# RWKV-7 scan on one Trainium2 core: carried state joined in PSUM by an identity product, new state written by ScalarE

## The chip, the cores and the metric

The kernel runs on one NeuronCore of one Trainium2 chip. The metric is the device time of one execution in microseconds (us), lower is better. Besides the timed executions there is one profiled execution, whose trace gives the start and length of every instruction on TensorE (PE for its matmuls, PEld for its weight loads), VectorE (DVE), ScalarE (ACT), GpSimd (POOL) and of the DMA queues issued by SyncE (SP).

## The reference, cut to what matters

The program is one step of a four-layer decoder trunk on 512 prompt tokens and 8 sample tokens, in float32. The second layer mixes tokens with RWKV-7: 16 heads, each with a 64x64 state matrix S that every token updates.

```python
def step(S, inp):
    r_t, w_t, k_t, v_t, kk_t, a_t = inp
    sa = jnp.einsum('bhvk,bhk->bhv', S, -kk_t)
    S = (S * w_t[:, :, None, :] + sa[..., None] * (kk_t * a_t)[:, :, None, :]
         + v_t[..., None] * k_t[:, :, None, :])
    return S, jnp.einsum('bhvk,bhk->bhv', S, r_t)

S, y = lax.scan(step, S0.astype(jnp.float32), (tm(rh), tm(decay), tm(kh), tm(vh), tm(kk), tm(ah)))
```

The other three layers (short convolution, gated linear attention, short convolution) and the feed-forward part behind each layer are not touched by the change.

## The kernel before, in words

**The scan.** The 512 prompt tokens are cut into 8 chunks of 64 (`NCH = 8`), and the 16 heads into two halves (`q` = 0 and 1) of four partition pairs: two heads of 64 channels lie one above the other in the 128 partitions, and index `i` runs over the four pairs. One scan step handles one chunk of one half, so there are 16 steps, numbered `w = 2 * c + q`. With decays taken relative to the start of a chunk, the step needs a triangular inverse of a 64x64 matrix per head, which it builds in five levels (2, 4, 8, 16, 32), then a right side, a solution `uu`, the outputs of the chunk and the new state.

**The rows of work.** TensorE's program is written out for all 16 steps. All its small products go through `both` (L2094), which issues one 64x64 matmul per head (line L2097 in the profile). In the trace every such float32 matmul shows as two records, so one call of `both` is four MATMUL records and four LDWEIGHTS records. Some products stay on the partitions they read ("diagonal"), others write the other head's partitions (`far`).

**One step in TensorE's order** (`scan_step`, L2203): the update products of level 0; the outputs of the previous step's solution (`outputs_of_solution`, rows `sc,uu`); the previous step's state sums (`state_products`, rows `uu,tok` and `tok`, eight calls of `both` into bank 7), which end with the semaphore `st_mm`; the first score products of the next step (rows `bd_B,bd_ZR`, `bd_ZR,bd_B`, `bd_ZR,bd_K`); the first products of level 1 (rows `mmt,ct`), and so on level by level.

**Around it.** In each level TensorE's first product (`t1_mm`) is copied out by ScalarE (`t`, L1405), TensorE makes the update products (rows `t,mmt` and `mmt,t`), VectorE adds them into `mmt` (L2920), and the next level's first products wait for that and for a masked matrix `ct` of GpSimd (L895). VectorE also masks the next step's scores (L2886), builds its operands (L2865, L2866, L2871, L2877) and walks through the sample tokens' state update (L2836 to L2850). GpSimd makes the next step's first inverse (L886, L888). ScalarE further writes the exponentials (L1363, L1364), `tok` (L1386, L1392), `uu` (L1433) and the outputs (L1436).

**The state.** `rw_ST` holds the state transposed. At the end of each step VectorE computes `st_end`, old state times end decay (L2942). When `st_mm` has come, VectorE writes the new state as (sums in bank 7) times end decay plus `st_end`, in four SCALAR_TENSOR_TENSOR (`update_state`, L2893), and copies the next end decay (`end_decays`, L2882), then waits for that copy before it masks the next scores.

**Order.** Each engine runs its instructions in the order in which the code writes them; only semaphores tie the engines together. There is no planner.

## Time and profile before

| | us |
|---|---|
| median of 3 timed runs | 3038.99 |
| lowest and highest | 3037.69, 3041.12 |
| span of the profiled execution | 3035.3 |
| the scan in it: first to last `rw_ST` write | 930.0 to 1133.6 |
| TensorE busy in the span | 2890.8 (95%) |
| VectorE busy | 1541.5 (51%) |
| ScalarE busy | 1051.5 (35%) |
| GpSimd busy | 1335.8 (44%) |

The trace gives no time of the profiled execution other than its span, first to last instruction; the median of the timed runs is 3.7 us above it.

In rows of the trace the first number is a start or a share as each heading says; `x4` is a count; `[0.24 <-PE banks L2097]` is idle time of the engine just before the row and what ended it. "issue" means that the engine waited for nothing that the profile shows. Consecutive instructions of an engine overlap, so the distance between starts, not the length, says what one costs in a row.

### The profile page before, as it was taken

The page shows a single profiled execution, that of the slowest core. Times are in us where ns is not written, and L with a number is a line of the kernel's source. Part 1 is how long each engine was busy: PE and PEld are TensorE (multiplying, and loading weights), DVE is VectorE, ACT ScalarE, POOL GpSimd, SP SyncE. Part 2 cuts the span into 40 slices and gives each one's busy share as a digit, 9 for nine tenths or more (in the row PEclk, how much of TensorE's full clock was granted, in tenths as well). Part 3 has the DMA queues.
Part 4 walks back from the last instruction along what each step waited for, and adds up shares of the span by engine and source line. Part 5 has one row for each costly group of instructions (what it writes and reads, how often), then busy time and mean ns, then how long its engine had stood idle before and what let it go on. Part 6 is the DMA issues. An engine that isn't in the chain of part 4 may idle for free.

```text
span 3035.3 us, 74569 instructions
## 1 busy us (share of the span) xinstructions
PE 2890.8 (95%) x30385; PEld 2739.4 (90%) x30385; DVE 1541.5 (51%) x2144; ACT 1051.5 (35%) x2059; POOL 1335.8 (44%) x981
## 2 busy tenths in 40 slices
PE   6998999998989899999998999989999999899998
PEld 6998999997978777899997899879999899799998
DVE  3435666128358884666603151476650444566612
ACT  4224333225454342433323443243332422433322
POOL 3443444442435564344443263434444344354443
PEclk8999999999999999999999899999999999899999
DMA  7544333543310014333344313433334443233332
GB/s 268 165 153 160 92 91 91 166 131 130 118 43 18 4 25 126 122 91 91 101 154 157 98 56 118 157 124 91 91 112 149 163 127 91 59 96 89 92 90 85
DMA packets 465625, 332.67 MB, mean 110 GB/s; under 512 B 19914, under 2 KB 435608, under 8 KB 465122
## 3 DMA queue, kind: packets, MB, share of 16 engines
q1 hardware_dynamic: 461400, 325.24, 34.5%
q10 hardware_dynamic: 4010, 4.22, 0.6%
q8 instruction: 178, 2.92, 0.4%
q14 instruction: 37, 0.30, 0.0%
HBM read 319.62 MB, written 10.20 MB: 109 GB/s over the span
## 4 chain that ended last, share of the span: by engine, by line
PE 57%; issue 4%; DVE 4%; POOL 3%; ACT 2%; DMA 1%; SPq 0%; POOLq 0%; ACTq 0%; DVEq 0%
PE banks L1638 33%; PE banks L1646 16%; POOL ct L895 2%; PE banks L2097 1%; PE banks L1599 1%; DVE h L2622 1%; PE banks L1944 1%; DVE proj L2566 1%; PE banks L1661 1%; POOL mmt L886 0%; PE banks L1732 0%; DMA s_state<-in_state_wkv_b_dram 0%; ACT conv L1074 0%; POOL mmt L888 0%; PE banks L2291 0%
## 5 line engine op out<-in xcount | busy, mean ns | idle before, releaser
L766 POOL TENSOR_TENSOR w_lo<-w_raw,w_hi 128x1024 fp32r<-128x1024 f32 x395 | 1007.3, 2551 | 1115.7 <-ACT w_hi L975 1095.7
L1638 PE MATMUL banks<-u_hi,w_hi 128*128 128x260 f32 x4064 | 836.8, 287 | 13.9 <-ACT w_hi L975 9.4
L1638 PE MATMUL banks<-u_lo,w_hi 128*128 128x260 f32 x4064 | 827.4, 285 | 0.0
L1638 PEld LDWEIGHTS banks<-u_hi,w_hi 128*128 128x128 f32 x4064 | 629.4, 190 | 27.1 <-issue 15.2
L1638 PEld LDWEIGHTS banks<-u_lo,w_hi 128*128 128x128 f32 x4064 | 632.1, 190 | 1.8
L975 ACT ACTIVATE w_hi<-w_raw 128x1024 fp32r<-128x1024 f32 x402 | 424.8, 1057 | 456.5 <-PE banks L1646 290.1
L1646 PE MATMUL banks<-u_hi,w_lo 128*128 128x260 f32 x4064 | 528.5, 283 | 0.0
L1646 PEld LDWEIGHTS banks<-u_hi,w_lo 128*128 128x128 f32 x4064 | 502.5, 187 | 1.8
L1638 PE MATMUL banks<-hid_hi,w_hi 128*128 128x260 f32 x1664 | 336.3, 283 | 0.0
L1638 PE MATMUL banks<-hid_lo,w_hi 128*128 128x260 f32 x1664 | 335.2, 283 | 0.0
L3069 DVE TENSOR_TENSOR csb<-proj 128x520 f32 (+1 forms) x42 | 30.3, 722 | 470.8 <-ACT proj L1042 470.8
L2554 DVE TENSOR_TENSOR hid_lo<-prod,hid_hi 128x520 f32 x104 | 261.6, 2516 | 12.8
L1638 PEld LDWEIGHTS banks<-hid_hi,w_hi 128*128 128x128 f32 x1664 | 256.8, 188 | 5.0 <-issue 3.7
L2538 DVE SCALAR_TENSOR_TENSOR conv<-gate,vecs,conv 128x536 f32<-128x536 f32 x104 | 249.1, 2395 | 15.1 <-DVE conv L2536 0.8
L1638 PEld LDWEIGHTS banks<-hid_lo,w_hi 128*128 128x128 f32 x1664 | 256.0, 188 | 0.0
L1646 PE MATMUL banks<-hid_hi,w_lo 128*128 128x260 f32 x1664 | 217.0, 282 | 0.0
L1646 PEld LDWEIGHTS banks<-hid_hi,w_lo 128*128 128x128 f32 x1664 | 206.4, 188 | 0.0
L781 POOL TENSOR_TENSOR tail<-gate,ones 128x2 f32<-128x2 f32 x104 | 27.1, 260 | 339.8 <-ACT gate L1507 339.8
L1514 ACT ACTIVATE conv<-conv,vecs 128x536 f32<-128x536 f32 x88 | 65.6, 745 | 287.5 <-DVE conv L2538 287.5
L2535 DVE TENSOR_SCALAR conv<-gate,vecs 128x536 f32<-128x536 f32 x104 | 56.0, 538 | 194.4 <-ACT gate L1507 190.3
L895 POOL TENSOR_TENSOR ct<-sc,head_up 128x128 f32<-128x128 f32 x160 | 92.3, 593 | 85.1 <-PE banks L2097 84.9
L1505 ACT ACTIVATE gate<-banks 128x260 f32<-128x260 f32 x88 | 34.1, 388 | 257.5 <-PE banks L1646 256.3
(461 smaller groups left out, 3903.9 us busy)
## 6 DMA issues: line engine op xcount, KB each, us to landing
w_raw<-in_ffn_w_up_dram SPq DMA_DIRECT2D x176, 512.0 KB, 3.6
ada_raw<-in_ada_w_dram SPq DMA_DIRECT2D x96, 512.0 KB, 4.8
w_raw<-in_ffn_w_down_dram SPq DMA_DIRECT2D x64, 448.0 KB, 3.8
w_raw<-in_sconv_w_in_dram SPq DMA_DIRECT2D x48, 512.0 KB, 5.3
ada_ahead<-in_ada_w_dram SPq DMA_DIRECT2D x36, 512.0 KB, 7.6
ada_ahead_down<-in_ada_w_dram SPq DMA_DIRECT2D x36, 512.0 KB, 6.4
w_raw<-in_ffn_w_down_dram SPq DMA_DIRECT2D x32, 512.0 KB, 4.1
ada_pro<-in_ada_w_dram SPq DMA_DIRECT2D x6, 2048.0 KB, 20.3
```

The source lines that it names most:

```text
L766: pool.tensor_tensor(w_lo[:, s, :, :], w_raw[:, s, :, :], w_hi[:, s, :, :].bitcast(F32), ALU.subtract).then_inc(lo_done, 1)
L895: pool.tensor_tensor(ct[:, 2 * g:2 * g + 2, :], sc[q][:, 2 * g:2 * g + 2, HD:2 * HD], m, ALU.mult).then_inc(ct_ready, 1)
L975: act.activation(w_hi[:, s, :, :], w_raw[:, s, :, :], ACT.Copy).then_inc(hi_done, 1)
L1505: act.activation(gate[:, e, 2:2 + HALF], tile_ps[0][0][:, 0:HALF], ACT.Copy)
L1514: act.activation(conv[:, e, 0:CWD], conv[:, e, 0:CWD], ACT.Silu, bias=vec("ffn_conv_b", l * FT + m)).then_inc(silu_done, 1)
L1599: mm = pe.matmul(acc_ps[g * QUAD:(g + 1) * QUAD, 0:2 * P], cT[:, k, :], parts[:, g, :, :], start=(k == 0), stop=(k == KT - 1))
L1638: pe.matmul(tile_ps[slot][half][0:width, 0:HALF], w_hi[:, s, k, 0:width], x[:, k0 + k, half * HALF:(half + 1) * HALF], start=start and k = ...
L1646: mm = pe.matmul(tile_ps[slot][half][0:width, 0:HALF], w_lo[:, s, k, 0:width], xh[:, k0 + k, half * HALF:(half + 1) * HALF], start=False, ...
L1661: pe.matmul(tile_ps[s][half][:, 0:HALF], w[:, s, k, :], xh[:, k, half * HALF:(half + 1) * HALF], start=(start and k == 0 and i == 0), stop ...
L2535: link(dve.tensor_scalar(conv[:, e, 0:CWD], gate[:, e, 0:CWD], w[0], None, ALU.mult))
L2538: dve.scalar_tensor_tensor(conv[:, e, 0:CWD], gate[:, e, 2:2 + CWD], w[2], conv[:, e, 0:CWD], ALU.mult, ALU.add).then_inc(conv_done, 1)
L2554: dve.tensor_tensor(lo, prod[:, e, :], hi.bitcast(F32), ALU.subtract).then_inc(hid_ready, 1)
```

## The change

Three things change in the scan. First, `state_products` on TensorE gets a third call of `both` per pair: identity times the old `rw_ST`, accumulated into the same sums in bank 7. Second, the new state is then those sums times the end decay alone; ScalarE writes it, as four ACTIVATE copies whose scale is a 128x1 column of `end_decay`, placed ahead of the level-1 copies of the step. Third, VectorE loses `st_end` and `update_state`; its copy of the end decay moves to level 2 of the step, behind a wait for `st_updated`, and signals a new semaphore `decays_ready`. ScalarE's loop is rewritten so that its first step stands outside.

```diff
-        st_end = at("st_end", [P, 4, HD], F32, big_off + 5 * 1024)
...
+                    def update_state(w, q):
+
+                        act.wait_ge(st_mm, w + 1)
+                        act.wait_ge(decays_ready, w + 1)
+                        for i in range(4):
+                            ins = act.activation(rw_ST[:, 4 * q + i, :], bank[7][:, i * HD:(i + 1) * HD], ACT.Copy,
+                                                 scale=end_decay[:, q, i:i + 1])
+                        ins.then_inc(st_updated, 1)
+
-                    def scan_step(c, q, one_more, two_more):
+                    def scan_step(c, q, one_more, two_more, first=False):
 
                         w = 2 * c + q
+                        if not first:
+                            update_state(w - 1, 1 - q)
                         for lvl in range(1, len(LEVELS)):
...
                             both(o, lambda rs: tok[q][rs, i, 0:HD], lambda rs: uu[rs, i, :], True, False)
-                            mm = both(o, lambda rs: tok[q][rs, i, HD:2 * HD], lambda rs: tok[q][rs, i, 2 * HD:3 * HD], False, True)
+                            both(o, lambda rs: tok[q][rs, i, HD:2 * HD], lambda rs: tok[q][rs, i, 2 * HD:3 * HD], False, False)
+                            mm = both(o, lambda rs: ident[rs, rs], lambda rs: rw_ST[rs, 4 * q + i, :], False, True)
                         mm.then_inc(st_mm, 1)
...
-                    def update_state(w, q, two_more):
-
-                        dve.wait_ge(st_mm, w + 1)
-                        for i in range(4):
-                            ins = dve.scalar_tensor_tensor(rw_ST[:, 4 * q + i, :], bank[7][:, i * HD:(i + 1) * HD],
-                                                           end_decay[:, q, i:i + 1], st_end[:, i, :],
-                                                           ALU.mult, ALU.add)
-                        ins.then_inc(st_updated, 1)
-                        if two_more:
-                            dve.wait_ge(st_updated, w + 3)
-                            link(end_decays(q))
...
-                            if lvl == 0 and not first:
-                                update_state(w - 1, 1 - q, one_more)
...
-                            elif lvl == 2 and two_more:
-                                dve.wait_ge(exp_done, w + 3)
-                                dve.wait_ge(rhs_mm, w + 1)
-                                build(c + 1, q)
+                            elif lvl == 2:
+                                if one_more and not first:
+                                    dve.wait_ge(st_updated, w + 2)
+                                    end_decays(1 - q).then_inc(decays_ready, 1)
+                                if two_more:
+                                    dve.wait_ge(exp_done, w + 3)
+                                    dve.wait_ge(rhs_mm, w + 1)
+                                    build(c + 1, q)
...
-                        dve.wait_ge(st_updated, w + 1)
-                        dve.wait_ge(st_updated, w + 2)
-                        link(dve.tensor_tensor(st_end[:, :, :], rw_ST[:, 4 * q:4 * q + 4, :],
-                                               end_decay[:, q, :].unsqueeze(2).to_broadcast([P, 4, HD]), ALU.mult))
```

On TensorE, in a step with q = 0, the state sums of the step before stood like this (each row of "x2" is one call of `both`, `uu` is the solution, `tok` keys and values, `bd_` rows are the scores that follow):

```order
L2097 MATMUL banks<-uu,tok_139 64x64 x2
L2097 MATMUL banks<-tok_139 64x64 x2
L2097 MATMUL banks<-uu,tok_139 64x64 x2
L2097 MATMUL banks<-tok_139 64x64 x2
L2097 MATMUL banks<-bd_B_123,bd_ZR_122 64x64 [waits bd_ready]
L2097 MATMUL banks<-bd_B_123,bd_ZR_122 64x64
L2097 MATMUL banks<-bd_ZR_122,bd_B_123 64x3x64 x2
L2097 MATMUL banks<-bd_ZR_122,bd_K_124 64x3x64 x2
L2097 MATMUL banks<-mmt_136,ct 64x64 [waits mmt_ready,ct_ready]
```

and in the changed program, where `both` is at L2110, the same place of a step reads:

```order
L2110 MATMUL banks<-uu,tok_139 64x64 x2
L2110 MATMUL banks<-tok_139 64x64 x2
L2110 MATMUL banks<-rw_ST,ident 64x64 x2
L2110 MATMUL banks<-uu,tok_139 64x64 x2
L2110 MATMUL banks<-tok_139 64x64 x2
L2110 MATMUL banks<-rw_ST,ident 64x64 x2
L2110 MATMUL banks<-bd_B_128,bd_ZR_127 64x64 [waits bd_ready]
L2110 MATMUL banks<-bd_B_128,bd_ZR_127 64x64
L2110 MATMUL banks<-bd_ZR_127,bd_B_128 64x3x64 x2
L2110 MATMUL banks<-bd_ZR_127,bd_K_129 64x3x64 x2
L2110 MATMUL banks<-mmt_134,ct 64x64 [waits mmt_ready,ct_ready]
```

Each pair has gained one call of `both` ahead of the scores and of the level-1 products (`mmt,ct`); nothing behind it changed its order.

On VectorE, behind the level-0 additions of a step, the program before has the new state, the end decay with its waits, then the first mask (`sc`) and the level-1 additions:

```order
L2920 TENSOR_TENSOR mmt_136<-mmt_136,banks 128x256 [waits tok_ready,d_mm]
L2893 SCALAR_TENSOR_TENSOR rw_ST<-banks,end_decay,st_end 128x64 [waits st_mm]
L2893 SCALAR_TENSOR_TENSOR rw_ST<-banks,end_decay,st_end 128x64 x3
L2898 REGISTER_ALU
L2882 COPY end_decay<-bd_Ep_126 128x4 [waits st_updated]
L2464 ISA
L2885 ISA [waits dve_step]
L2886 TENSOR_TENSOR sc_133<-banks,sc_mask 128x320 [waits sc_done]
```

and the changed program goes from the additions to the mask at once:

```order
L2921 TENSOR_TENSOR mmt_135<-mmt_135,banks 128x256 [waits tok_ready,d_mm]
L2898 ISA
L2899 TENSOR_TENSOR sc_132<-banks,sc_mask 128x320 [waits sc_done]
L2909 REGISTER_ALU
L2921 TENSOR_TENSOR mmt_135<-mmt_135,banks 128x256 [waits mmt_ready,d_mm]
```

The end decay's copy has moved two levels down, between the mask and the operands of level 2.

On ScalarE, the program before goes from the outputs' copy (`rw_kk`) to the level-1 copies (`t`):

```order
L1436 ISA [waits y_mm]
L1436 ACTIVATE rw_kk<-banks 128x4x64
L1404 REGISTER_ALU
L1405 ACTIVATE t_138<-banks 128x128 [waits t1_mm]
L1404 REGISTER_ALU
L1405 ACTIVATE t_138<-banks 128x128 [waits t1_mm]
```

and the changed program has the new state between them:

```order
L1446 ISA [waits y_mm]
L1446 ACTIVATE rw_kk<-banks 128x4x64
L1410 REGISTER_ALU
L1413 ACTIVATE rw_ST<-banks,end_decay 128x64 [waits decays_ready,st_mm]
L1413 ACTIVATE rw_ST<-banks,end_decay 128x64 x3
L1403 ISA
L1404 ACTIVATE t_137<-banks 128x128 [waits t1_mm]
```

So the level-1 copies now stand behind a wait for `st_mm` and four more instructions.

## Rows read from the trace of the kernel before

**Rows 1.** The page, part 1, busy time and share of each engine.
```profile
PE 2890.8 (95%) x30385; PEld 2739.4 (90%) x30385; DVE 1541.5 (51%) x2144; ACT 1051.5 (35%) x2059; POOL 1335.8 (44%) x981
```

**Rows 2.** Busy time by stretch, the 15 scan steps, columns as headed.
```profile
core 0: us, PE busy (x) PEld busy (x) DVE busy (x) ACT busy (x) POOL busy (x), PEclk, DMA share, GB/s
926.00:1133.00 207.00, 188.78 (x6487) 169.24 (x6479) 174.88 (x422) 86.48 (x319) 125.22 (x212) 0.99 0.02 6
```

**Rows 3.** Waits in the same stretch: waiter, releaser, us in total, times, longest.
```profile
PEld banks L2097 <- issue: 20.5, 41, 1.8
DVE rw_ST L2893 <- PE banks L2097: 8.7, 16, 1.4
PE banks L2097 <- POOL mmt L888: 5.2, 7, 0.9
PE banks L2097 <- DVE mmt L2920: 2.6, 4, 1.7
PEld banks L2097 <- ACT t L1405: 1.4, 7, 0.2
```

**Rows 4.** PE's timeline in one step: start, length, instruction, count, idle before.
```profile
981.83 0.25 PE L2097 MATMUL banks<-sc,uu 64*64 64x64 f32 x1
...
982.33 0.22 PE L2097 MATMUL banks<-uu,tok 64*64 64x64 f32 x1
...
983.26 0.22 PE L2097 MATMUL banks<-bd_B,bd_ZR 64*64 64x64 f32 x1
...
983.45 0.27 PE L2097 MATMUL banks<-mmt,ct 64*64 64x64 f32 x2
```

**Rows 5.** DVE's timeline in the same step.
```profile
982.30 0.74 DVE L2920 TENSOR_TENSOR mmt<-mmt,banks 128x256 f32<-128x256 f32 x2
983.54 0.86 DVE L2893 SCALAR_TENSOR_TENSOR rw_ST<-banks,end_decay,st_end 128x64 f32<-128x64 f32 x4 [0.50 <-PE banks L2097]
984.43 0.17 DVE L2882 COPY end_decay<-bd_Ep 128x4 f32<-128x4 f32 x1
984.76 0.49 DVE L2886 TENSOR_TENSOR sc<-banks,sc_mask 128x320 f32<-128x320 f32 x1 [0.16 <-DVE end_decay L2882]
985.49 0.75 DVE L2920 TENSOR_TENSOR mmt<-mmt,banks 128x256 f32<-128x256 f32 x2 [0.24 <-PE banks L2097]
```

**Rows 6.** ACT's timeline in the same step, solution and level-1 copies.
```profile
981.30 0.38 ACT L1433 ACTIVATE uu<-banks 128x256 f32<-128x256 f32 x1 [0.20 <-PE banks L2097]
984.40 0.45 ACT L1405 ACTIVATE t<-banks 128x128 f32<-128x128 f32 x2 [1.32 <-PE banks L2097]
```

**Rows 7.** ACT's lengths by line: ns min/median/max; copies without and with a column scale.
```profile
L1386 ACT ACTIVATE tok<-banks x64: 266/273/285, 908.8 to 1114.4; 128x128 f32<-128x128 f32 x64
L1398 ACT ACTIVATE mmt<-banks x16: 384/384/386, 913.9 to 1116.0; 128x256 f32<-128x256 f32 x16
L1424 ACT ACTIVATE bonus_ones<-pair_ones,vecs x8: 389/392/403, 1119.6 to 1126.7; 128x128 f32<-128x128 f32 x8
```

**Rows 8.** ACT's timeline, last step: two scaled copies in a row.
```profile
1119.27 0.48 ACT L1405 ACTIVATE t<-banks 128x128 f32<-128x128 f32 x2 [0.64 <-PE banks L2097]
1119.64 0.68 ACT L1424 ACTIVATE bonus_ones<-pair_ones,vecs 128x128 f32<-128x128 f32 x2
```

**Rows 9.** DVE's timeline, last step: its own new state.
```profile
1119.18 0.86 DVE L2893 SCALAR_TENSOR_TENSOR rw_ST<-banks,end_decay,st_end 128x64 f32<-128x64 f32 x4 [1.05 <-PE banks L2097]
```

**Rows 10.** DMA queues in 926 to 1133: packets, MB, share.
```profile
q8 instruction: 52, 0.85, 1.6%
```

**Rows 11.** Timeline behind the scan, PE.
```profile
1130.88 0.42 PE L2097 MATMUL banks<-uu,tok 64*64 64x64 f32 x4
...
1132.65 1.98 PE L2283 MATMUL banks<-rw_kk,pair_ones 128*128 128x512 f32 x4
...
1134.73 1.10 PE L2097 MATMUL banks<-ident,rw_ST 64*64 64x64 f32 x32
```

**Rows 12.** DVE's length of the old state's product, ns min/median/max.
```profile
L2942 DVE TENSOR_TENSOR st_end<-rw_ST,end_decay x16: 410/420/1105, 926.5 to 1128.7; 128x256 f32<-128x256 f32 x16
```

**Rows 13.** GpSimd's first inverse, a step with q = 1, then one with q = 0.
```profile
964.51 0.90 POOL L886 TENSOR_TENSOR mmt<-sc,low_mask 128x128 f32<-128x128 f32 x1
965.50 0.78 POOL L888 TENSOR_TENSOR mmt<-mmt,head_ident 128x128 f32<-128x128 f32 x1
...
978.70 0.45 POOL L886 TENSOR_TENSOR mmt<-sc,low_mask 128x128 f32<-128x128 f32 x1
979.23 0.46 POOL L888 TENSOR_TENSOR mmt<-mmt,head_ident 128x128 f32<-128x128 f32 x1
```

More of the change, by code:

```diff
@@ L347, in trunk_kernel @@
         scores_masked = sem("scores_masked")
-        exp_done, bd_ready, keys_built = sem("exp_done"), sem("bd_ready"), sem("keys_built")
+        exp_done, bd_ready, decays_ready = sem("exp_done"), sem("bd_ready"), sem("decays_ready")
         sc_done, tok_done, tok_ready = sem("sc_done"), sem("tok_done"), sem("tok_ready")
@@ L1447, in _ @@
                        .then_inc(srow_copied, 1)
-                    with act.Fori(0, NCH - 1) as c:
-                        for q in range(2):
-                            scan_step(c, q, True, True)
+                    scan_step(0, 0, True, True, first=True)
+                    with act.Fori(0, NCH - 2) as c:
+                        scan_step(c, 1, True, True)
+                        scan_step(c + 1, 0, True, True)
+                    scan_step(NCH - 2, 1, True, True)
                     for q in range(2):
                         scan_step(NCH - 1, q, q == 0, False)
+                    update_state(2 * NCH - 1, 1)
                     act.dma_start(g2[:, :], A["rwkv_g2"][0]).then_inc(g2_loaded, 16)
@@ L2870, in build_rates @@
                         b, qs, now = bd[q], slice(4 * q, 4 * q + 4), ds(HD * c, HD)
-                        dve.tensor_tensor(b["B"][:, :, :], rw_b[:, qs, now], b["Em"][:, :, :], ALU.mult)\
-                           .then_inc(keys_built, 1)
+                        dve.tensor_tensor(b["B"][:, :, :], rw_b[:, qs, now], b["Em"][:, :, :], ALU.mult)
                     def receptances(c, q):
@@ L2951, in _ @@
                         receptances(0, q)
-                        link(end_decays(q))
+                        end_decays(q).then_inc(decays_ready, 1)
                     for i in range(4):
@@ L2957, in _ @@
                     scan_step(0, 0, first=True)
-                    b0, s0, PER = base[0], step[0], 2 * 2 + 9
+                    b0, s0, PER = base[0], step[0], 9
                     with dve.Fori(0, NCH - 2) as c:
@@ L2967, in _ @@
                     scan_step(NCH - 1, 1, one_more=False, two_more=False)
-                    update_state(2 * NCH - 1, 1, False)
                     dve.wait_ge(dve_step, base[0] + step[0])
```

## The prediction, made before the changed kernel ran

> **What bounds the kernel now.** I read the page's busy shares first: TensorE 95%, the others 35 to 51% [rows 1]. The change touches only the RWKV scan, so I cut out its stretch, 926 to 1133 us. There TensorE is busy 188.8 of 207 us and VectorE 174.9 of 207 [rows 2]. Both look full, and the whole question is which of them sets the pace where the state is handed over: work is taken from VectorE and put on TensorE and ScalarE.
>
> Next the waits of that stretch [rows 3]. VectorE waits for TensorE before every write of `rw_ST`, 8.7 us in 16 times; TensorE waits for VectorE's `mmt` only 4 times, 2.6 us. The reader should see that VectorE is early where the change relieves it. "Issue" on the weight loads (20.5 us) I come back to.
>
> Then one step on three engines. ScalarE delivers `uu` at 981.68 [rows 6]. From there TensorE runs without a gap: solution products, state sums from 982.33, scores from 983.26, level-1 products (`mmt,ct`) from 983.45 [rows 4]. What those last wait for from VectorE, the level-0 `mmt`, was complete at 983.04 [rows 5], its first half some 0.3 us earlier, since the two take 0.74. So TensorE's own row of work decides, not VectorE. The new state starts on VectorE at 983.54, as soon as the sums are there, after 0.50 us of idling, and the level-1 copies start on ScalarE at 984.40, that is 0.86 us after the sums [rows 5, 6]. The level-1 additions at 985.49 again follow idle time that TensorE ended [rows 5].
>
> **The change part by part.**
>
> *Identity products, on TensorE.* The eight calls of `both` in the state sums take 982.33 to 983.26, 0.93 us, 0.116 each [rows 4]. Four more of the same shape are 0.465 us, and they stand ahead of the scores, of the level-1 products and of `st_mm`. Nothing in this stretch waits for anyone else, so nothing hides them. Steps 1 to 15 have them: 15 x 0.465 = 7.0 us. The last state sums, behind the scan, run slower, 1130.88 to 1132.65 for eight [rows 11], 0.22 each: +0.9 us, in front of the mean products of the next part. Together +7.9. Bounds: nothing, if they run beside other products; 16 x 0.9 = 14 us, if at the rate of the last ones everywhere.
>
> The Trainium skill, page "TensorEngine Tiling (Array Packing)", section "Key Properties", says that tiles operate independently and can load weights and multiply in parallel. The identity products are on the diagonal tiles and the `mmt,ct` products on the other two, so by that rule these could start beside them, which is a rival below. The trace agrees only in part: `mmt,ct` starts 0.19 us after the first score record, before the scores are through, but it did not start at 983.04, when its inputs were there [rows 4, 5].
>
> *The new state, on ScalarE.* No four such instructions are in the trace. A copy of 128 elements from PSUM takes 273 ns and one of 256 takes 384, so 64 elements fewer are worth 0.055 us; one with a column scale takes 392 for 128 [rows 7]. Two of those in a row take 0.68, so the distance between starts is 0.29 [rows 8], and for 64 elements about 0.24. Four hold ScalarE 0.94 us after `st_mm`; the level-1 copies were due 0.86 us after it. They are 0.08 late, of which I count half, since TensorE still has the right side and scores to run: 14 x 0.04 = 0.6 us. Lower bound 0: copies without a scale have a distance of 0.21 at most (two in 0.48, the length 0.27 of one taken off [rows 7, 8]), so four are through in 0.84. Upper bound: no overlap at all, 4 x 0.34 = 1.35, late by 0.49, 14 x 0.49 = 6.9 us. I take the value from the scaled rows, the nearest.
>
> Step 15 has no scores between the sums and the level-1 products, so its copies start 0.09 us after `st_mm` (1119.27 against 1119.18 [rows 8, 9]) and will be 0.85 late: I take +0.7, from 0 to 0.9. Behind the scan the new state ends 0.94 after the sums, and TensorE spends 1.98 us on mean products before it reads `rw_ST` [rows 11]: nothing.
>
> *What VectorE loses.* `st_end`, 0.42 us and its wait [rows 12]; the four writes and the wait for the end decay, from 983.54 to the mask at 984.76 [rows 5]. That is 1.2 + 0.5 = 1.7 us per step, 25 us of its time in all. It pays nothing where VectorE idles before and after. What is late next in its place is TensorE: the first mask then waits for its scores, the level-1 additions for TensorE's update products as now. At most the additions come 0.1 us sooner where they now follow the mask directly (6 of 15 steps): 0 to -0.6, I take 0.
>
> *The moved end decay.* One copy of 0.17 us [rows 5], now ahead of the operands of level 2, behind a wait for a state that ScalarE has written two levels earlier. It delays the level-3 additions by about 0.1 us; TensorE is then still in scores and past outputs. Zero; if that cover is gone, 14 x 0.1 = 1.4.
>
> *Instructions fetched.* 52 packets of code arrive in 207 us, in which TensorE executes 12966 records [rows 2, 10]: 249 records each. 128 more matmuls are 512 records (each shows as two products and two loads), two packets more. The unexplained gaps are 20.5 us, 0.39 per packet [rows 3, 10]: +0.8. Bounds: 0, and 5 either way if the gaps fall on other places.
>
> Sum: 7.9 + 0.6 + 0.7 + 0.8 = 10.0 us. The profiled execution would have a span of 3035.3 + 10.0 = 3045.3; the median of the timed runs is 3.7 above the span, so 3049.0 us (+0.33%). About 0.2%, 6.1 us, is what a measurement of this kernel can tell from no change.
>
> **The rivals.**
>
> *Hidden products (3041).* TensorE issues products on idle tiles past waiting ones, so the identity products lie beside `mmt,ct`, as the rule of the skill would have it, and ScalarE fits. For: `mmt,ct` overlaps the scores by some records [rows 4]. Against: it began 0.41 us after VectorE was done. What stays is step 15 and the code, +1.5, so 3040.5 to 3041. Chance 0.17.
>
> *ScalarE takes the place of VectorE as the late one (3056).* Its four writes don't overlap: 1.35 us, level-1 copies 0.49 late in every step. Sum 7.9 + 6.9 + 0.7 + 0.8 = 16.3, so 3055.3. Against: two scaled copies in a row do overlap [rows 8]. Chance 0.10.
>
> *VectorE was the bound after all (faster, 3022).* Place: the mask and level-1 additions behind `st_mm`, and `st_end` ahead of the level-0 additions. Price: all 1.7 us per step are on the path, 15 x 1.7 = 25 off against 8 on: -17, so 3022. It decides from the point at which the level-0 `mmt` ends later than the state sums and scores do. For: VectorE is busy 84% of the scan. Against: the 0.41 us of margin at level 0 and the idle time before `rw_ST` and before the additions [rows 5]. Chance 0.05.
>
> *GpSimd gets quicker (3044).* In steps with q = 1 its inverse takes 0.90 and 0.78 us where it takes 0.45 and 0.46 with q = 0 [rows 13], and TensorE waits 5.2 us for it in 7 times [rows 3]. The slow ones lie beside VectorE's sample-state work; if the freed VectorE no longer meets them, up to 5.2 us come back: 3043.8. Against: no removed instruction stands in levels 3 and 4. Chance 0.08.
>
> *The code gaps fall otherwise.* 5 us more or less: 3044 or 3054. Chance 0.08.
>
> **How the numbers follow.** Forecast (7 to 13 us slower, 3046 to 3052) 0.52, the rivals 0.17, 0.10, 0.05, 0.08 and 0.08. The range: from the hidden products at 3040 to ScalarE's case at 3056. Slower by over 0.2% (above 3045.1): 0.50 of the forecast, 0.10 of ScalarE, 0.04 of the code gaps, 0.64. Faster by over 0.2% (below 3032.9): VectorE's 0.05 and 0.03 for part of it together with hidden products, 0.08. Within: 0.28.
>
> **What would show it.** In each step, the start of the solution products to the first `mmt,ct` should grow from 1.6 to 2.1 us, with VectorE's level-0 additions done some 0.9 us before. Four ScalarE writes should span about 1.05 us and the first `t` follow 0.9 to 1.0 after the first of them. VectorE should show some 25 us less work and more idle time released by TensorE. GpSimd's 0.90 and 0.78 should stay. I am wrong if the distance from solution products to `mmt,ct` stays at 1.6 (hidden products), if `t` starts over 1.2 us after `st_mm` (ScalarE), or if the steps get shorter at all.

## The result, and the profile after

| | before | changed |
|---|---|---|
| timed median, same chip, us | 3037.69 (5 runs, 3036.57 to 3041.12) | 3047.47 (5 runs, 3045.82 to 3057.34) |
| ratio | | 1.0039, 95% interval 1.0028 to 1.0049 |
| span of the profiled execution, us | 3035.3 | 3055.6 |

The changed kernel is slower by 9.8 us where 10.0 were forecast, and 1.5 us under the forecast time of 3049.0, which was built on a median of before of 3038.99. Its profiled execution was the longest of its five (3057.34 timed), so its span must not be set beside that of before. The span lies 1.7 us under the time of the same execution; the 3.7 us of the prediction compared the span of one execution with the median of others.

The profile after, part 1, busy time and share of each engine (for [rows 1]):

```profile
PE 2905.9 (95%) x30641; PEld 2751.9 (90%) x30641; DVE 1520.8 (50%) x2064; ACT 1063.3 (35%) x2123; POOL 1330.9 (44%) x981
```

TensorE has 256 matmul records more (16 steps, 4 calls of `both`, 4 records each), VectorE 80 instructions and 20.7 us less. The same stretch as in [rows 2], columns as there:

```profile
926.00:1133.00 207.00, 187.39 (x6385) 168.06 (x6383) 146.10 (x332) 91.39 (x356) 113.19 (x202) 1.00 0.02 4
```

VectorE fell from 174.9 to 146.1 us, partly because the stretch now ends before the scan does; TensorE is busy for about as long as before (187.4 us, it was 188.8). Now the waits of 926 to 1150, since the changed scan ends at 1150 (waiter, releaser, us, times, longest; for [rows 3]):

```profile
DVE sc L2899 <- PE banks L2110: 37.4, 15, 3.3
DVE mmt L2921 <- PE banks L2110: 26.8, 39, 3.0
PEld banks L2110 <- issue: 23.7, 46, 1.8
ACT rw_ST L1413 <- PE banks L2110: 20.4, 16, 2.1
PE banks L2110 <- issue: 12.0, 25, 1.0
```

VectorE's freed time shows here as waits for TensorE, before the first mask (`sc`) and the additions (`mmt`). ScalarE waits 20.4 us for the sums: taken together, it is early at `rw_ST`, not late.

One step of the changed kernel (q = 0, as in [rows 4]) on TensorE: start, length, instruction, count; `...` marks rows left out here and below.

```profile
1105.27 0.68 PE L2110 MATMUL banks<-sc,uu 64*64 64x64 f32 x16
1105.78 0.28 PE L2110 MATMUL banks<-uu,tok 64*64 64x64 f32 x4
1105.90 0.28 PE L2110 MATMUL banks<-tok 64*64 64x64 f32 x4
1106.02 0.28 PE L2110 MATMUL banks<-rw_ST,ident 64*64 64x64 f32 x4
...
1107.18 0.28 PE L2110 MATMUL banks<-bd_B,bd_ZR 64*64 64x64 f32 x4
...
1107.31 0.33 PE L2110 MATMUL banks<-mmt,ct 64*64 64x64 f32 x4
```

Starts are 0.117 us apart, call after call, with the identity product (`rw_ST,ident`) as one of three. From the first solution product to the first `mmt,ct` it is 2.04 us; before it was 1.58 in most steps without a gap and 1.62 in the one shown [rows 4]. That is the four calls, 0.47 us. Five of the 15 steps of each of the first two traces have this 2.04; nine of the others, at 2.45 to 3.28, nearly all hold a gap of TensorE that nothing explains, and the last step went from 1.23 to 1.65. `mmt,ct` starts 0.13 us after the first score, as it did at 0.19 before, but in this step not beside the identity products; only in the last step, which has no scores, does it start 0.10 us ahead of the last of them. The rule that tiles work independently (Trainium skill, page "TensorEngine Tiling (Array Packing)", section "Key Properties") would have let it; the trace shows it in part only, here as before.

VectorE and ScalarE in the same step (for [rows 5, 6]), VectorE first:

```profile
1105.14 0.74 DVE L2921 TENSOR_TENSOR mmt<-mmt,banks 128x256 f32<-128x256 f32 x2
1108.16 0.49 DVE L2899 TENSOR_TENSOR sc<-banks,sc_mask 128x320 f32<-128x320 f32 x1 [2.28 <-PE banks L2110]
1109.52 0.75 DVE L2921 TENSOR_TENSOR mmt<-mmt,banks 128x256 f32<-128x256 f32 x2 [0.86 <-PE banks L2110]
```

```profile
1107.40 0.93 ACT L1413 ACTIVATE rw_ST<-banks,end_decay 128x64 f32<-128x64 f32 x4 [0.94 <-PE banks L2110]
1108.26 0.45 ACT L1404 ACTIVATE t<-banks 128x128 f32<-128x128 f32 x2
```

The level-0 additions are over at 1105.88, 1.43 us before `mmt,ct`; VectorE idles 2.28 us and then 0.86 us. The four ScalarE writes take 0.93, and the first `t` starts 0.86 us after the first of them, the very distance at which `t` followed the sums before [rows 5, 6]. It is 0.86 in 12 of the 14 steps that have scores, before and after the change. So ScalarE is not late. In the last step it is (ScalarE, then TensorE's first update product):

```profile
1135.27 0.93 ACT L1413 ACTIVATE rw_ST<-banks,end_decay 128x64 f32<-128x64 f32 x4 [1.02 <-PE banks L2110]
1136.07 0.46 ACT L1404 ACTIVATE t<-banks 128x128 f32<-128x128 f32 x2
```

```profile
1136.41 0.27 PE L2110 MATMUL banks<-t,mmt 64*64 64x64 f32 x2 [0.43 <-ACT t L1404]
```

The copies start 0.80 us after the sums instead of 0.09 [rows 8, 9], and TensorE waits 0.43 us for them. In the kernel before, TensorE had an idle time of 0.51 us in the same place that nothing explains (two traces), so the additions, 1.80 us behind the sums then, are 1.68 behind them now: the lateness is there, but no more than 0.43 us of it can be on the path. All 64 writes (ns min/median/max, first and last start):

```profile
L1413 ACT ACTIVATE rw_ST<-banks,end_decay x64: 304/314/324, 931.6 to 1150.1; 128x64 f32<-128x64 f32 x64
```

The length is 314 ns, and between starts lie (0.93 - 0.31) / 3 = 0.206 us, where 0.24 was estimated. The last state sums, behind the scan (for [rows 11]), first and last call and what follows:

```profile
1146.71 0.42 PE L2110 MATMUL banks<-uu,tok 64*64 64x64 f32 x4
...
1149.06 0.35 PE L2110 MATMUL banks<-rw_ST,ident 64*64 64x64 f32 x4
1149.34 1.98 PE L2297 MATMUL banks<-rw_kk,pair_ones 128*128 128x512 f32 x4
```

2.63 us to the mean products instead of 1.77: +0.86, against 0.9 forecast.

### The profile page after: what moved, and what is told of

Same layout as the page of the kernel before. It is cut to its first block, busy times and chain, and to the rows that moved or that the text cites. A ratio compares the mean times of both kernels' runs of the same rounds, so it can differ in the third digit from the quotient of the medians.

```text
span 3055.6 us, 75024 instructions
## 1 busy us (share of the span) xinstructions
PE 2905.9 (95%) x30641; PEld 2751.9 (90%) x30641; DVE 1520.8 (50%) x2064; ACT 1063.3 (35%) x2123; POOL 1330.9 (44%) x981
## 4 chain that ended last, share of the span: by engine, by line
PE 57%; issue 5%; DVE 3%; POOL 3%; ACT 2%; DMA 1%; SPq 0%; POOLq 0%; ACTq 0%; DVEq 0%
PE banks L1651 33%; PE banks L1659 16%; POOL ct L894 2%; PE banks L1612 1%; PE banks L1674 1%; PE banks L1957 1%; DVE h L2636 1%; PE banks L2110 1%; DVE proj L2580 1%; POOL mmt L885 1%; PE banks L1745 0%; PE banks L1680 0%; DMA s_state<-in_state_wkv_b_dram 0%; DMA w_raw<-in_ffn_w_up_dram 0%; POOL mmt L887 0%
## 5 line engine op out<-in xcount | busy, mean ns | idle before, releaser
L1659 PE MATMUL banks<-hid_hi,w_lo 128*128 128x260 f32 x1664 | 217.0, 282 | 0.0
L2549 DVE TENSOR_SCALAR conv<-gate,vecs 128x536 f32<-128x536 f32 x104 | 56.0, 538 | 195.8 <-ACT gate L1520 191.8
```

What stands on the lines that cost most here:

```text
L1659: mm = pe.matmul(tile_ps[slot][half][0:width, 0:HALF], w_lo[:, s, k, 0:width], xh[:, k0 + k, half * HALF:(half + 1) * HALF], start=False, ...
L2549: link(dve.tensor_scalar(conv[:, e, 0:CWD], gate[:, e, 0:CWD], w[0], None, ALU.mult))
```

## What was tested, and how the scan is read

Two theories. **A**: TensorE's own row of work sets the pace where the state is handed over; the identity products cost their full length, about 7 us and 0.9 for the last, and the exchange of VectorE against ScalarE costs next to nothing. **B**: a good part of the 10 us is another edit, above all the end decay's copy at level 2, and the identity products are partly hidden.

Single executions of one kernel differ by several us, in the scan mostly by TensorE's idle time that ends with "issue". So I read from each trace the time from the first to the last state write ("scan"), TensorE's "issue" idle time in it, and the difference ("rest"). This stretch holds 14 of the 15 groups of identity products in the steps, and the last one behind them. These are the two kinds of rows, for the kernel before (its writes, and waits in 930.0 to 1133.4):

```profile
L2893 DVE SCALAR_TENSOR_TENSOR rw_ST<-banks,end_decay,st_end x64: 270/276/288, 930.0 to 1133.4; 128x64 f32<-128x64 f32 x64
```

```profile
PE banks L2097 <- issue: 8.5, 17, 1.0
```

| kernel | scan, us | "issue" | rest | timed median, us (runs) | ratio, 95% interval |
|---|---|---|---|---|---|
| before | 203.4 | 8.5 | 194.9 | 3037.69 (5) | |
| before, again | 205.0 | 11.7 | 193.3 | 3036.56 (1) | |
| changed | 218.5 | 12.0 | 206.5 | 3047.47 (5) | 1.0028 to 1.0049 |
| changed, again | 217.0 | 12.5 | 204.5 | 3047.02 (7) | 1.0018 to 1.0040 |
| changed, third time | 213.2 | 8.9 | 204.3 | 3048.42 (8) | 1.0023 to 1.0046 |
| identity products alone | 214.8 | 13.4 | 201.4 | 3047.10 (12) | 1.0013 to 1.0033 |
| changed without them | 208.8 | 11.3 | 197.5 | 3037.44 (11) | 0.9992 to 1.0011 |
| the same again | 206.7 | 9.8 | 196.9 | 3034.92 (1) | |
| identity at the step's end | 215.4 | 16.8 | 198.6 | 3043.08 (11) | 1.0002 to 1.0020 |
| changed, end decay late | 213.0 | 10.9 | 202.1 | 3043.41 (12) | 1.0015 to 1.0034 |
| the same again | 212.0 | 9.7 | 202.3 | 3044.02 (12) | 1.0014 to 1.0031 |
| before, copy at level 2 | 206.7 | 10.0 | 196.7 | 3037.19 (12) | 0.9993 to 1.0013 |
| before, scores later | 205.8 | 14.0 | 191.8 | 3039.43 (12) | 0.9999 to 1.0017 |

The kernel before, run beside them, had medians of 3039.05 (31 runs; changed again, both identity kernels, changed without them), 3036.50 (23; end decay late, copy at level 2, the repeats) and 3037.07 (25; changed third time, end decay late again, scores later).

The "rest" repeats within 2.2 us for the three changed runs, within 1.6 for before and 0.6 for the others that ran twice; the "issue" time of one and the same kernel runs from 8.9 to 12.5. Averages: before 194.1, changed 205.1, so +11.0. Differences of 2 us between two rests are no more than scatter.

## The experiments

**The changed kernel again.** No edit.

> The changed kernel once more, for a profile whose time lies nearer the median (the first one's span, 3055.6 us, was the slowest of five). Theory A (TensorE's row of work sets the pace and the identity products lengthen it by 0.465 us per step): the distance from the solution products to the level-1 products is 2.04 us in steps without a gap, as in the first profile, the timed median is 3045 to 3050 us, and what differs between executions is the sum of the unexplained gaps on TensorE (12.0 us against 8.5 before). Rival B (ScalarE's new instructions are late): the level-1 copies start over 1.0 us after the first state write.

Measured: 3047.02 us, ratio 1.0029; the step from solution products to `mmt,ct` as in the first trace, and the level-1 copies 0.86 us behind the first state write. Theory A's numbers came out, rival B's sign did not.

**Identity products alone.** The kernel before, with the four calls ahead of each pair's sums; the sums then overwrite them, and VectorE still adds the old state.

```diff
                         for i in range(4):
                             o = lambda rs: bank[7][rs, i * HD:(i + 1) * HD]
+                            both(o, lambda rs: ident[rs, rs], lambda rs: rw_ST[rs, 4 * q + i, :])
                             both(o, lambda rs: tok[q][rs, i, 0:HD], lambda rs: uu[rs, i, :], True, False)
```

> The kernel before with four identity products added ahead of the state sums; they are overwritten by the sums, so the state is computed as before on VectorE. Theory A: +7.9 us for the products and up to +1 for the code that is fetched, 3046 to 3047 us, nearly all that the whole change costs. Rival B (ScalarE's part or the moved waits cost it): under +4. Rival C (products hidden on idle tiles): under +2.

Measured: 3047.10 us, ratio 1.0023; beside it the changed kernel had 3047.02. The rest of the scan is +7.3 us (201.4 against 194.1), where 14 x 0.465 and 0.9 for the last would be 7.4. The products alone cost what the forecast says.

**The changed kernel without them.** The sums lack the old state.

```diff
-                            both(o, lambda rs: tok[q][rs, i, HD:2 * HD], lambda rs: tok[q][rs, i, 2 * HD:3 * HD], False, False)
-                            mm = both(o, lambda rs: ident[rs, rs], lambda rs: rw_ST[rs, 4 * q + i, :], False, True)
+                            mm = both(o, lambda rs: tok[q][rs, i, HD:2 * HD], lambda rs: tok[q][rs, i, 2 * HD:3 * HD], False, True)
```

> The changed kernel without the identity products: the old state is left out of the new one, all else (state written by ScalarE, VectorE relieved, end decay moved) is as changed. Theory A: within 2 us of the kernel before, 3037 to 3040, since VectorE's 25 us were not on the path and ScalarE is in time; solution products to level-1 products back at 1.58 us. Rival B: +4 or more. Rival D (relief of VectorE is worth something that the products ate up): 3030 or less.

Measured: 3037.44 us, ratio 1.0001, as theory A expected. VectorE has lost its 1.7 us per step here too, and nothing came of it; that VectorE was the bound has fallen. Its waits (926 to 1150) show where the time went:

```profile
DVE sc L2898 <- PE banks L2110: 28.2, 14, 3.1
ACT rw_ST L1413 <- PE banks L2110: 10.8, 16, 1.8
```

The traces show the rest of the scan at 197.2 on average, +3.1, which the time does not tell from nothing (its interval reaches from -2.4 to +3.3 us). Those 3 us were not in the forecast; the runs from "the end decay's copy" on are about them.

**Identity products at the step's end.** The kernel before, with the four calls after the step's outputs of the past, behind which TensorE waits for GpSimd's inverse. They signal `keys_built` in place of VectorE's last operand, and TensorE waits for that ahead of the inverse's products.

```diff
+                    def old_state(q):
+                        for i in range(4):
+                            mm = both(lambda rs: bank[7][rs, i * HD:(i + 1) * HD], lambda rs: ident[rs, rs],
+                                      lambda rs: rw_ST[rs, 4 * q + i, :])
+                        mm.then_inc(keys_built, 1)
...
+                        old_state(q)
...
+                            pe.wait_ge(keys_built, w + 1)
```

> As e1, but the four identity products stand at the end of the step, between the level-4 update products and the turned values, where TensorE waits 0.4 to 0.9 us for GpSimd's first inverse in steps with q = 1. Theory A: hidden in those steps, full price in the others: 8 x 0.465 = 3.7, with the last and the code +5 us, 3042 to 3043. Rival: if the fetched code is the price and not TensorE's time, the same as e1, +8 to +9.

Measured: 3043.08 us, ratio 1.0011; rest of the scan +4.5. By the medians 4 us of the 8 are hidden when the same work stands beside a wait, by the rests 2.8 of the 7.3. The intervals of the two ratios overlap (1.0002 to 1.0020 and 1.0013 to 1.0033), so the size is rough. TensorE's waits in the scan, first with the products ahead of the sums (930.1 to 1144.9), then at the end (931.6 to 1147.0):

```profile
PE banks L2097 <- POOL mmt L888: 4.2, 6, 0.9
PE banks L2097 <- DVE mmt L2921: 2.9, 4, 1.7
```

```profile
PE banks L2097 <- issue: 16.8, 33, 1.2
PE banks L2097 <- DVE mmt L2929: 1.9, 3, 1.3
PE banks L2097 <- POOL mmt L888: 1.4, 4, 0.4
```

The wait for GpSimd shrank from 4.2 to 1.4 us: 2.8 us of cover, and the rest differs by 2.8 (201.4 against 198.6). The "issue" time is the largest of all runs, so that its scan is no shorter than that of the products alone, although its time is: the part behind the scan varies too, by some us, and one trace can't tell a difference of 3 us in the whole.

**The kernel before, and the changed one without identity products, again.** No edit; one execution each, to see how far one trace repeats.

> The kernel before, once more, for a second profile of its scan: in the first one the scan took 202.8 us from the first to the last state write. If that one was typical, 201 to 205 again, with about 17 gaps on TensorE; if it was a lucky one, 206 or more. Level 2's to level 3's additions on VectorE 2.01 us apart where VectorE doesn't idle.

> The changed kernel without the identity products (the old state is left out) once more: its scan took 208.2 us in the first profile although its timed median was that of the kernel before. If the moved end decay costs 0.33 us per step (level 2's to level 3's additions 2.35 us apart), 207 to 209 again, 4 to 5 above the kernel before; if the difference was chance, the two lie within 2 us of each other.

Measured: scans of 205.0 and 206.7 us, rests of 193.3 and 196.9. The scans are 1.7 us apart, within the 2 us that the expectation called chance; in the rests the 3 us stay, but they are only twice the scatter.

**The end decay's copy, late.** The changed kernel, with VectorE's copy moved from ahead of the operands of level 2 to where `st_end` had stood.

```diff
                             elif lvl == 2:
-                                if one_more and not first:
-                                    dve.wait_ge(st_updated, w + 2)
-                                    end_decays(1 - q).then_inc(decays_ready, 1)
...
+                        if one_more and not first:
+                            dve.wait_ge(st_updated, w + 2)
+                            end_decays(1 - q).then_inc(decays_ready, 1)
```

> The changed kernel with the copy of the end decay moved from level 2 to the end of the step, where st_end used to stand. Theory E (the small copy delays VectorE's operands of level 2 by 0.07 us, and the first of them then runs beside GpSimd and takes 0.69 instead of 0.41; together 0.34 per step, on the path): additions of level 3 at 2.01 us behind those of level 2, and 3 to 5 us off the changed kernel, 3042 to 3044. Rival (as predicted: the copy is hidden): the same as the changed kernel, 3047.

Measured: 3043.41 us. From the level-2 to the level-3 additions it is 2.01 us again in most steps, where the changed kernel takes 2.35. VectorE there, changed kernel (third run), then with the late copy:

```profile
992.73 0.75 DVE L2921 TENSOR_TENSOR mmt<-mmt,banks 128x256 f32<-128x256 f32 x2 [1.20 <-PE banks L2110]
993.40 0.48 DVE L2899 TENSOR_TENSOR sc<-banks,sc_mask 128x320 f32<-128x320 f32 x1
993.80 0.16 DVE L2895 COPY end_decay<-bd_Ep 128x4 f32<-128x4 f32 x1
993.87 0.69 DVE L2879 TENSOR_TENSOR bd_ZR<-rw_kk,bd_Ep 128x256 f32<-128x256 f32 x1
...
995.08 0.74 DVE L2921 TENSOR_TENSOR mmt<-mmt,banks 128x256 f32<-128x256 f32 x2
```

```profile
990.82 0.75 DVE L2921 TENSOR_TENSOR mmt<-mmt,banks 128x256 f32<-128x256 f32 x2 [0.92 <-PE banks L2110]
991.49 0.48 DVE L2899 TENSOR_TENSOR sc<-banks,sc_mask 128x320 f32<-128x320 f32 x1
991.89 0.41 DVE L2879 TENSOR_TENSOR bd_ZR<-rw_kk,bd_Ep 128x256 f32<-128x256 f32 x1
...
992.82 0.74 DVE L2921 TENSOR_TENSOR mmt<-mmt,banks 128x256 f32<-128x256 f32 x2
```

The copy itself moves the next start by 0.07 us; the first operand, `bd_ZR`, then takes 0.69 instead of 0.41. The additions follow straight behind the operands in both, so in this step VectorE's row is what decides, and the copy adds 0.34 us.

**A copy at level 2 alone.** The kernel before, with one more copy of 128x4 into a spare tile ahead of the operands.

```diff
+                                dve.tensor_copy(spare[:, :], bd[1 - q]["Ep"][:, :, HD:HD + 1].rearrange("p i a -> p (i a)"))
```

> The kernel before with one more copy of 128x4 elements on VectorE ahead of the operands of level 2, into a tile that nobody reads; nothing else changed. Theory E: 0.34 us per step in 14 steps, +4 to +5 us, 3042 to 3043, with the first operand at 0.69 us. Rival (hidden): within 1 us of the kernel before.

Measured: 3037.19 us, ratio 1.0003, 0.7 us above the kernel before. The 4 to 5 us that theory E expected did not come; the interval, 0.9993 to 1.0013, leaves room for up to 4 us and for nothing at all. In the trace the additions are 2.35 us or more apart in every step, and the rest of the scan is 196.7, +2.6. First the kernel before, VectorE and GpSimd, then the one with the copy:

```profile
987.40 0.76 DVE L2920 TENSOR_TENSOR mmt<-mmt,banks 128x256 f32<-128x256 f32 x2 [0.16 <-PE banks L2097]
...
988.47 0.42 DVE L2865 TENSOR_TENSOR bd_ZR<-rw_kk,bd_Ep 128x256 f32<-128x256 f32 x1
...
989.83 0.75 DVE L2920 TENSOR_TENSOR mmt<-mmt,banks 128x256 f32<-128x256 f32 x2 [0.35 <-PE banks L2097]
```

```profile
988.47 0.73 POOL L888 TENSOR_TENSOR mmt<-mmt,head_ident 128x128 f32<-128x128 f32 x1
```

```profile
989.72 0.75 DVE L2921 TENSOR_TENSOR mmt<-mmt,banks 128x256 f32<-128x256 f32 x2 [0.16 <-PE banks L2098]
...
990.86 0.68 DVE L2866 TENSOR_TENSOR bd_ZR<-rw_kk,bd_Ep 128x256 f32<-128x256 f32 x1
...
992.15 0.75 DVE L2921 TENSOR_TENSOR mmt<-mmt,banks 128x256 f32<-128x256 f32 x2
```

```profile
990.78 0.48 POOL L889 TENSOR_TENSOR mmt<-mmt,head_ident 128x128 f32<-128x128 f32 x1
```

These rows show two things. The first is why the whole 0.34 us is not paid in every step. Here the additions are 2.43 us apart in both kernels, because in the kernel before they waited 0.35 us for TensorE; the copy filled idle time. In each trace of the kernel before, 8 of 13 steps have the additions within 2.1 us; the others wait for TensorE or have their operand slowed by GpSimd already. On average over the 13 steps the distance is 2.23 and 2.27 us before, 2.49 with the copy and 2.51 and 2.47 in the changed kernel without identity products: 0.24 us per step or 3.1 us. It is 2.45, 2.42 and 2.47 in the changed kernel and 2.20 and 2.12 with the late end decay: 0.28 us or 3.7.

The second is GpSimd. Without the copy the operand and GpSimd's operation start together, VectorE takes 0.42 and GpSimd 0.73. With it GpSimd starts 0.08 first, takes 0.48, and VectorE takes 0.68. The same holds for the first operand in all 13 traces, 169 cases. In the 77 in which GpSimd's operation (`mmt` or `ct`) starts between 0.016 us ahead of VectorE's and 0.032 behind it, VectorE takes 0.41 to 0.42 and GpSimd 0.70 to 0.75. In the 72 in which GpSimd is 0.035 to 0.088 ahead, GpSimd takes 0.45 to 0.49 and VectorE 0.65 to 0.70. In the other 20 the two starts lie further apart and VectorE takes 0.41 to 0.59.

The Trainium skill, page "SBUF — State Buffer", section "Who interferes with whom", says that a VectorE instruction with two inputs in SBUF contends with a GpSimd instruction that reads SBUF, and that the order of issue decides which of them is blocked. These rows agree: both of the operand's inputs lie in SBUF, and some 0.27 us changed sides with the order of the starts. The loser lost 0.24 to 0.29 us; waiting for the other's end would have cost VectorE 0.40 here.

**Changed kernel and late end decay on one chip.** No new edit: the two were timed beside each other.

> The changed kernel, unchanged, to be timed beside the kernel with the late end decay on the same chip. Each profile of it so far took 8 to 10 us longer than the kernel before; forecast 3046.5 us. If the chip of this batch is as the others, the theory (identity products cost 15 x 0.465 = 7.0 us, the rest of the change next to nothing) and the rival (identity products 7, the moved end decay 3 more, something given back elsewhere) say the same here.

> The changed kernel with the end decay's copy back behind the level-3 additions. In its first profile the additions of levels 2 and 3 stood 2.01 us apart instead of 2.35. Theory A, the 0.34 us per step are on the path of 14 steps, 4.8 us: this kernel is 4 to 5 us faster than the changed kernel of the same batch, about 3042. Theory B, TensorE has scores and past outputs to do there, so most of it is hidden: at most 1.5 us faster, about 3045.5. I hold the two for equally likely, since the first timing (3043.4) was made on another occasion than those of the changed kernel (3047.0 and 3047.5).

Measured: 3048.42 and 3044.02 us, 4.4 apart; ratios to before of 1.0035 and 1.0022. The changed kernel came 1.9 us above its forecast. The late one is 4.4 us faster, as theory A of its expectation said, but lies at 3044.0, between the two theories' times. The intervals (1.0023 to 1.0046, 1.0014 to 1.0031) overlap: resampling the 8 and 12 times gives 3.2 us for the difference of the means, 95% of it from 0.3 to 5.9, and for that of the medians from -1.2 to 6.6. The rests of the scans say 2.9 (205.1 against 202.2). I take 3 us for the moved copy, an estimate that rests on the traces and that the times bear out only from 0 to 6. The mean length of the 13 first operands in 926 to 1133, late kernel:

```profile
L2879 DVE TENSOR_TENSOR bd_ZR<-rw_kk,bd_Ep 128x256 f32<-128x256 f32 x13 | 5.7, 435 | 0.0
```

In the changed kernel the same 13 take 648 ns.

**The next scores later.** The kernel before, with the next step's first scores behind the first products of level 1.

```diff
-                        if one_more:
-                            scores_among(w + 1, qn, 0)
-                            scores_of_keys(w + 1, qn, 0)
...
+                            if one_more and lvl == 1:
+                                scores_among(w + 1, qn, 0)
+                                scores_of_keys(w + 1, qn, 0)
```

> The kernel before with the next step's first scores (four calls, about 0.2 us of TensorE's row) moved from ahead of the level-1 first products to behind them. Theory, TensorE's whole row of work sets the pace around the state sums: an order changes nothing that must be done, so the time stays within 2 us of the kernel before, about 3038, unless the row behind is waiting. Rival, it is the latency chain solution, state sums, scores, level-1 products, level-1 copies, update products, additions that sets it, and TensorE idles behind it: the level-1 products come 0.2 us sooner in 15 steps, so 3 us faster, about 3035, and the identity products then cost because they lie in that chain, not because TensorE is full. The mask of the scores comes later in this kernel, which may cost VectorE's first addition up to 0.2 us per step.

Measured: 3039.43 us, ratio 1.0008, 0.9999 to 1.0017: 2.4 us above the kernel before, a little outside what the theory allows, and not the 3 us gain of the rival. One step, VectorE, ScalarE, TensorE:

```profile
984.38 0.86 DVE L2893 SCALAR_TENSOR_TENSOR rw_ST<-banks,end_decay,st_end 128x64 f32<-128x64 f32 x4 [0.50 <-PE banks L2097]
...
986.44 0.75 DVE L2920 TENSOR_TENSOR mmt<-mmt,banks 128x256 f32<-128x256 f32 x2 [0.36 <-PE banks L2097]
```

```profile
984.47 0.48 ACT L1405 ACTIVATE t<-banks 128x128 f32<-128x128 f32 x2 [0.55 <-PE banks L2097]
```

```profile
986.03 0.27 PE L2097 MATMUL banks<-t,mmt 64*64 64x64 f32 x2 [0.26 <-issue]
```

The level-1 copies now start 0.09 us after the sums instead of 0.86, but the additions follow 2.06 us after them, where it was 1.95 [rows 5]. In between TensorE has 0.26 us of unexplained idle time, which the step of before has not. So the latency has to be read in steps without such a gap. The kernel before, then the one with the scores later:

```profile
1040.09 0.86 DVE L2893 SCALAR_TENSOR_TENSOR rw_ST<-banks,end_decay,st_end 128x64 f32<-128x64 f32 x4 [0.58 <-PE banks L2097]
...
1041.87 0.75 DVE L2920 TENSOR_TENSOR mmt<-mmt,banks 128x256 f32<-128x256 f32 x2
```

```profile
1041.89 0.86 DVE L2893 SCALAR_TENSOR_TENSOR rw_ST<-banks,end_decay,st_end 128x64 f32<-128x64 f32 x4 [0.30 <-PE banks L2097]
...
1043.52 0.74 DVE L2920 TENSOR_TENSOR mmt<-mmt,banks 128x256 f32<-128x256 f32 x2
```

Here the additions come 1.63 us after the sums instead of 1.78; the four steps without a gap have 1.57 to 1.69 where the same steps of before have 1.79, and the rest of the scan is 2.3 us shorter than before. So the traces point to a gain of 0.1 to 0.2 us per step, as the rival said, which an "issue" time of 14.0 us instead of some 10 ate in this execution; the times of twelve show no gain. Whether the identity products cost their length because TensorE's row is full or because they lie in the chain from the solution to the level-1 additions is therefore not settled by this run. They lie in both.

## Why the prediction was right, step by step

**Identity products, 7.0 + 0.9.** Right, size and place. 0.47 us per step in the trace, 0.86 behind the scan, +7.3 in the rest of the scan and 8 us in time for the products alone. The rival of hidden products had its sign in the distance to `mmt,ct`, which grew to 2.04 where no gap lies in it. Only where TensorE waits anyway were they hidden, by a third to a half. That "nothing hides them" because TensorE's row is full is the prediction's reason; the runs show the price, and leave open how much of it is the row and how much the chain ("the next scores later").

**ScalarE's writes, 0.6, and step 15, 0.7.** The first was over-sized: distance 0.206 us and not 0.24, so the four span 0.93 us instead of 1.05, the copies come at 0.86 instead of 0.9 to 1.0, and it is 0. In step 15 the copies are 0.71 us late, as forecast, but TensorE waits only 0.43 us for them, so the second is at most 0.4. Identity products and ScalarE together, which is the changed kernel with the late end decay, have a rest of 202.2, 0.8 above the products alone, which the scatter does not tell from 0.4. The rival of late ScalarE has fallen.

**VectorE's relief, 0.** Right. VectorE is busy 20.7 us less in the whole execution (some 25 with its waits were forecast), its waits for TensorE ahead of the first mask have grown from 1.2 to 37.4 us, and without the identity products the ratio is 1.0001.

**The moved end decay, 0.** Wrong by its size: about 3 us by the traces. The step that failed is "it delays the level-3 additions by about 0.1 us; TensorE is then still in scores and past outputs". The copy delays them by 0.34 us, since the operand behind it loses its start to GpSimd, and only about a third of that is covered: 13 x 0.34 = 4.4 (the copy of w = 14 has no operands behind it), of which 2.6 to 3.1 show in the rests. The upper bound of 1.4 was too low, because it took the copy's price from its own length alone. The times bear this out only weakly: on average the changed kernel is 9.7 us above before and the late end decay 6.9, so 2.8, but the copy by itself shows 0.7, and the changed kernel without identity products nothing.

**Instructions fetched, +0.8.** The two more packets of code came (180 instead of 178 in the page), but their price is not to be told: the "issue" time of the changed kernel was 12.0, 12.5 and 8.9 us in three executions, that of before 8.5 and 11.7. The prediction priced a packet by the 20.5 us for which the weight loads idled [rows 3]; TensorE's products idled 8.5 us with "issue", which would be 0.16 us per packet and 0.3 in all. That the gaps come from the code at all is shown by no run.

**GpSimd quicker.** Did not happen: its 0.90 and 0.78 us are still there, in seven steps as before, and TensorE waits 4.6 to 4.9 us for it in 6 times, before 5.2 in 7 and 4.7 in 6.

**The sum.** 7.9 + 0.4 + 3 = 11.3 by parts, of which 10.8 lie in the stretch of the table; the rest of the scan shows 11.0, and the timed differences are 9.8, 8.0 and 11.4. The main term was right in price and place. That the total came within 0.2 us was luck: 0.9 us too much at ScalarE and 0.8 at the gaps stood against some 3 us too few at the end decay, and the three timings lie 3.4 us apart.

## What to carry to other kernels

Here, work moved from an engine with idle time before and after it to the engine whose row is full cost its whole length there and returned nothing, even where the relieved engine is busy for 84% of the stretch; what mattered is who ends its idle time. When work must go on the full engine, put it where that engine waits, and read a latency only in steps without an unexplained gap. And price a small instruction ahead of others by what it does to the start of the next one beside a neighbour engine, not by its own length.

## What the runs showed of the hardware that was not expected

- A copy of 0.16 us on VectorE cost 0.34 where the additions follow directly: the operand behind it went from 0.41 to 0.69 us, and GpSimd's operation beside it from 0.73 to 0.48, when GpSimd's started 0.08 us ahead instead of together with it.
- Four ScalarE copies of 128x64 from PSUM with a column scale: 314 ns each, 0.206 us between starts.
- With the scores moved behind it in the program, `mmt,ct` started 1.27 us after the first solution product instead of 1.62, beside the last state sums; standing behind them, it had started 0.41 us after its inputs were ready.
- TensorE's idle time without a visible releaser scatters by some 4 us in 215 from one execution of a kernel to the next (8.9 to 12.5), more than several of the terms that a sum of this kind carries.
